# Prompt output summed in PSUM, gather from unscaled rows, and expert weights in transfers of 2 MB: a hybrid decoder step with a mixture of experts

## The reference, cut to what matters

```python
x = x + mix
x = x + moe(rmsnorm(x, norm_ffn_g), ...)     # then y = rmsnorm(x, norm_final_g)

logits = x2 @ w_router + b_router            # x2 is the normalised row, (288, 1024)
top_vals, top_idx = lax.top_k(logits, 4); gates = softmax(top_vals)
# rows sorted by expert, in blocks; each block with its expert's weights:
gu = xb @ w_up[e] + b_up[e]                  # w_up[e]: (1024, 2048)
gate, up = gu[:, :1024], gu[:, 1024:]
gate = minimum(gate, 7); up = clip(up, -7, 7)
act = (up + 1) * (gate * sigmoid(1.702 * gate))
out = act @ w_down[e] + b_down[e]            # w_down[e]: (1024, 1024)
y = segment_sum(out * row_gate, row_tok)
```

## Time and profile before

| what | value |
|---|---|
| runs | 1273.46 us median of 3 (1272.34 to 1274.46) |
| the profiled execution | 1271.02 us, with a span of 1269.2 us |
| busy | PE 1152.5 us (91%), DVE 676.7 (53%), POOL 653.9 (52%), ACT 244.0 (19%) |
| transfers | 448.91 MB (decimal), mean 354 GB/s over the span |
| mean granted clock of PE | 0.972 |

### The profile page before, as it was taken

One profiled execution on the slowest core, in us unless ns is written; L12 is line 12 of the kernel. 1 busy time (PEld: TensorE's weight loads), 2 busy tenths in 40 slices (PEclk: granted clock), 3 DMA queues, 4 the chain that ended last, 5 costly groups with the idle time before them and its releaser, 6 DMA issues.

```text
span 1269.2 us, 30932 instructions
## 1 busy us (share of the span) xinstructions
PE 1152.5 (91%) x11113; PEld 586.8 (46%) x11114; DVE 676.7 (53%) x1256; ACT 244.0 (19%) x487; POOL 653.9 (52%) x709
## 2 busy tenths in 40 slices
PE   8999999999999989799797998997997879979895
PEld 7777777775444334243332443432433324434332
DVE  2999984121755635545342557553554445535534
ACT  2012124001222212122121221221221212212122
POOL 1012300000566858749671687586585756857863
PEclk9999999999999999999898999998998989989998
DMA  9974443336999999999999799999999999999996
GB/s 263 349 242 129 163 129 117 114 142 278 380 385 397 396 422 422 421 422 422 422 422 422 282 400 424 422 422 422 422 422 422 422 422 422 422 422 422 422 422 277
DMA packets 94539, 448.91 MB, mean 354 GB/s; under 512 B 8502, under 2 KB 42870, under 8 KB 45315
## 3 DMA queue, kind: packets, MB, share of 16 engines
q1 hardware_dynamic: 94078, 447.21, 87.8%
q10 hardware_dynamic: 437, 1.39, 0.3%
HBM read 447.00 MB, written 2.42 MB: 354 GB/s over the span
## 4 chain that ended last, share of the span: by engine, by line
PE 60%; DMA 18%; DVE 17%; issue 3%; DVEq 1%; ACT 1%; POOL 0%; SPq 0%; POOLq 0%; ACTq 0%
PE banks L1372 21%; DMA ring<-in_w_down 17%; PE banks L1382 13%; DVE staging L803 8%; PE banks L1167 8%; PE banks L1089 5%; PE banks L1147 4%; PE banks L1126 3%; PE banks L1283 2%; PE banks L1133 2%; PE banks L1156 1%; DMA staging<-in_w_up 1%; DVE hT L1036 1%; DVE hT L1029 1%; DVE staging L812 1%
## 5 line engine op out<-in xcount | busy, mean ns | idle before, releaser
L524 POOL COPY ring<-staging 128x1024 f32<-128x1024 f32 x620 | 623.8, 1053 | 472.0 <-PE banks L1372 372.4
L1372 PE MATMUL banks<-ring,hT 128*32 128x512 f32 x3328 | 414.8, 604 | 12.7 <-DVE hT L779 7.5
L330 DVE TENSOR_TENSOR xt<-xt,banks 128x1024 f32<-128x1024 f32 x106 | 128.7, 1215 | 371.7 <-PE banks L1147 371.7
L1382 PE MATMUL banks<-ring,hT 128*32 128x256 f32 x3328 | 229.1, 395 | 73.3 <-DMA ring<-in_w_down 64.4
L1382 PEld LDWEIGHTS banks<-ring,hT 128*32 128x32 f32 x3328 | 109.6, 114 | 249.7 <-issue 136.3
L1167 PE MATMUL banks<-hT,ring 128*128 128x288 f32 x768 | 188.4, 406 | 0.3 <-ACT hT L561 0.3
L1372 PEld LDWEIGHTS banks<-ring,hT 128*32 128x32 f32 x3328 | 104.8, 111 | 149.9 <-issue 106.8
L1167 PEld LDWEIGHTS banks<-hT,ring 128*128 128x128 f32 x768 | 145.1, 190 | 39.7 <-issue 0.4
L683 ACT COPY WT<-banks 128x256 f32<-128x256 f32 x52 | 19.4, 372 | 533.8 <-PE banks L1382 533.8
L803 DVE SCALAR_TENSOR_TENSOR staging<-staging 128x256 f32<-128x256 f32 x240 | 107.4, 522 | 0.0
L762 DVE TENSOR_SCALAR WT<-slot_ids,prod 128x32 f32 x156 | 81.5, 581 | 0.0
(11 more groups left out here) (245 smaller groups left out, 737.0 us busy)
## 6 DMA issues: line engine op xcount, KB each, us to landing
staging<-in_w_up SPq DMA_DIRECT2D x248, 1024.0 KB, 18.5
ring<-in_w_down SPq DMA_DIRECT2D x66, 1024.0 KB, 11.1
staging<-in_w_down SPq DMA_DIRECT2D x62, 1024.0 KB, 18.4
ring<-in_w_in SPq DMA_DIRECT2D x24, 1024.0 KB, 10.3
ring<-in_w_up SPq DMA_DIRECT2D x8, 1024.0 KB, 4.8
ring<-in_w_branch_b SPq DMA_DIRECT2D x4, 1024.0 KB, 5.4
ring<-in_w_branch_a SPq DMA_DIRECT2D x4, 1024.0 KB, 4.9
ring<-in_w_out SPq DMA_DIRECT2D x4, 1024.0 KB, 5.0
```

Of the source, the lines that this page charges most:

```text
L330: nc.vector.tensor_tensor(dst, dst, rows, ALU.add).then_inc(y_added, 1)
L524: ins = nc.gpsimd.tensor_copy(ring[:, k, half], staged[k][:, half])
L1372: ins = mm(UP[g * BLK:(g + 1) * BLK, :], xT[:, k, :], ring[:, k, g * 512:(g + 1) * 512], start=k == 0, stop=k == UP_SLOTS - 1)
L1382: ins = mm(DN[q * BLK:(q + 1) * BLK, 0:256], actT[:, f % 4, f // 4, :], ring[:, UP_SLOTS + j, h * D + q * 256:h * D + (q + 1) * 256], star ...
```

## The change

1. **Transfers.** Two neighbouring slots become one unit of 2 MB, loaded by one transfer with runs of 16 KB: two rows of `w_up`, or four rows of `w_down`, for each partition. There are six units for an expert; units 0 to 4 go through `staging`, unit 5 (slots 10 and 11) is loaded into the ring. POOL still copies a slot at a time, from a unit that has landed whole; it counts 8 for each half on `unit_full`. SP's order is kept: units 0 to 2 of the place after, unit 5 of this place, units 3 and 4. Since a partition now holds rows 2p and 2p+1 of a unit, the transposes of the gathered rows take every second element, and those of `raw` and `b_up` every fourth; `norm_ffn_g` is loaded a second time, as four rows of 256, and turned into a ninth column set (`FFN_PAIRS`) for `take_x`.
2. **Prompt output.** Banks 4 to 7 hold the prompt's output through the whole expert loop. PE starts them with an identity times `xt` (`start_rows`), every `combine` adds to them, and the last one ends the sum. DVE's adds to `xt` and PE's waits for them leave; only the sample's add stays (`add_sample`). The tail's squares and scales read PSUM.
3. **Gather.** `stage` no longer holds scaled rows for the prompt: the 0/1 matrix is multiplied with the reciprocal, and the gather reads `xt`.

```diff
@@ staging @@
-        staged = [staging[:, u, h * SLOT:(h + 1) * SLOT] for u in range(STAGED) for h in range(2)]
+        staged = [staging[:, u, :] for u in range(STAGED)]
...
@@ sync @@
+            load(ffn_rows[:], a["norm_ffn_g"][0].rearrange("(q n) -> q n", q=QN), vec_in)
...
-            def load_slot(e, k):
-                sp.dma_start(ring[:, k, :], slot_source(e, k)).then_inc(slot_full[k], 16)
...
-            def load_last_slots(e, before):
-                for k in range(2 * STAGED, SLOTS):
-                    sp.wait_ge(down_used, before * DOWN_SLOTS + (k - UP_SLOTS + 1))
-                    load_slot(e, k)
+            def unit_source(e, u):
+                if u < UP_UNITS:
+                    return a["w_up"][0, bass.ds(e, 1), u * 256:(u + 1) * 256, :].rearrange("e (p h) n -> p (e h n)", p=P)
+                lo = (u - UP_UNITS) * 512
+                return a["w_down"][0, bass.ds(e, 1), lo:lo + 512, :].rearrange("e (p h) n -> p (e h n)", p=P)
+            def load_unit(e, u):
+                sp.dma_start(ring[:, 2 * u:2 * u + 2, :].rearrange("p s n -> p (s n)"), unit_source(e, u)
+                             ).then_inc(unit_full[u], 16)
+            def load_staged_again(place, after, us):
+                for u in us:
+                    sp.wait_ge(unit_full[u], place * 16 + 16)
+                    load_staged(after, u)
+            def load_last_unit(e, before):
+                sp.wait_ge(down_used, before * DOWN_SLOTS + DOWN_SLOTS)
+                load_unit(e, UNITS - 1)
...
-                load_staged_again(place, after, range(2 * AHEAD))
-                load_last_slots(here, before)
-                load_staged_again(place, after, range(2 * AHEAD, 2 * STAGED))
+                load_staged_again(place, after, range(AHEAD))
+                load_last_unit(here, before)
+                load_staged_again(place, after, range(AHEAD, STAGED))
@@ gpsimd @@
+                for u in range(UP_UNITS):
+                    pool.wait_ge(staged_full[u], place * 16)
+                    for h in range(2):
+                        pool.wait_ge(up_used, before * UP_SLOTS + (2 * u + h + 1))
+                        copy_slot(u, h)
...
@@ scalar, tail @@
+            act.wait_ge(rows_combined, 1)
             for tt in range(2):
-                act.wait_ge(y_added, bodies * NT + (NT + tt + 1))
-                nc.scalar.activation(stage[:, tt, :], xt[:, tt, :], ACT.Square, accum_out=ss[:, tt:tt + 1]
+                nc.scalar.activation(squares[tt], y_rows[tt], ACT.Square, accum_out=ss[:, tt:tt + 1]
                                      ).then_inc(squared3, 1)
-                act.wait_ge(squared3, tt + 1)
-                root(ss[:, 4 + tt:5 + tt], ss[:, tt:tt + 1], 1.0 / D, rooted2)
+            act.wait_ge(squared3, 2)
+            root(ss[:, 4:6], ss[:, 0:2], 1.0 / D, rooted2)
@@ vector @@
+                for tt in range(2):
+                    V.tensor_scalar(sel[:, tt, :], slot_ids[:, bass.ds(rank0, BLK)],
+                                    rankm[:, tt, bass.ds(expert, 1)], ss[:, 4 + tt:5 + tt], ALU.is_equal, ALU.mult)
...
-                    V.tensor_scalar(stage[:, tt, :], xt[:, tt, :], col2, None, ALU.mult).then_inc(rows_kept, 1)
...
-                add_before(i, 2)
+                add_sample(i)
                 dve.wait_ge(combT_turned, i + 1)
                 select_weighted(column1)
                 dve.wait_ge(gathered, i + 2)
                 select(column2)
-                add_before(i, 1)
-                dve.wait_ge(combined, i * NT + (NT + 1))
-                add_output(dve, row_out[0], 0)
@@ tensor @@
+                pairs = xg.rearrange("r (p h) -> r h p", h=2)
                 for h in range(2):
-                    ins = tr(turned[:, h], xg[:, h * P:(h + 1) * P])
+                    ins = tr(turned[:, h], pairs[:, h])
...
+            def start_rows():
+                for q in range(QN):
+                    mm(bank[4 + q].rearrange("p (t n) -> p t n", t=2), ident[:], x_cols[:, q], start=True, stop=False)
+            def combine(tt, last=False):
+                for q in range(QN):
+                    ins = mm(y_rows[tt][:, q, :],
                              combT[q * BLK:(q + 1) * BLK, tt * P:(tt + 1) * P],
-                             out_sb[q * BLK:(q + 1) * BLK, :], start=True, stop=True)
+                             out_sb[q * BLK:(q + 1) * BLK, :], start=False, stop=last)
...
-                pairs = raw.rearrange("t (b p h) -> t b h p", h=2, p=P)
+                fours = raw.rearrange("t (p c) -> t c p", c=4)
                 for c in range(4):
-                    ins = tr(TB[:, c * P:(c + 1) * P], pairs[:, c // 2, c % 2])
+                    ins = tr(TB[:, c * P:(c + 1) * P], fours[:, c])
...
                 for k in range(UP_SLOTS):
-                    up(k, after)
+                    up(k, after + 8, after + 16)
                     if k == 2:
                         pe.wait_ge(act_ready, i + 1)
-                        pe.wait_ge(y_added, i * NT + 2)
+                        pe.wait_ge(sample_added, i + 1)
                     if 2 <= k < 2 + DOWN_SLOTS:
-                        down(k - 2, here)
+                        down(k - 2, here + 8, here + 16)
                 pe.wait_ge(combT_ready, i + 2)
                 pe.wait_ge(out_ready, i + 1)
-                pe.wait_ge(y_added, i * NT + NT)
-                combine(0, row_out[0])
+                combine(0)
```

More of the change, by code:

```diff
@@ L185, in carve @@
             return regs[region][0:rows, lo:lo + n]
+        squares = [regs["hT"][:, tt * D:(tt + 1) * D].rearrange("p (q n) -> p q n", q=QN) for tt in range(2)]
         xT = carve("hT", KC * BLK).rearrange("p (k t) -> p k t", k=KC)
@@ L213, in hybrid_layer @@
         UP, TB, XB, DN = bank[0:4]
[L214 to L217, removed]
+        high = banks[:, 4:8, :]
+        y_rows = (high[:, :, 0:256], high[:, :, 256:512])
+        sample_out = DN[:, 256:512]
         slot_full = [sem(f"slot_full{k}") for k in range(SLOTS)]
-        staged_full = [sem(f"staged_full{k}") for k in range(2 * STAGED)]
+        unit_full = [sem(f"unit_full{u}") for u in range(UNITS)]
+        staged_full = [sem(f"staged_full{u}") for u in range(STAGED)]
         slot_free = sem("slot_free")
@@ L390, in _ @@
                 load_block(n)
[L392 to L397, removed]
-            def load_slot(e, k):
-                sp.dma_start(ring[:, k, :], slot_source(e, k)).then_inc(slot_full[k], 16)
-            def load_staged(e, k):
-                sp.dma_start(staged[k], slot_source(e, k)).then_inc(staged_full[k], 16)
@@ L428, in _ @@
-            for k in range(UP_SLOTS, 2 * STAGED):
-                load_staged(1, k)
+            for u in range(UP_UNITS, UNITS):
+                load_unit(0, u)
+            load_staged(1, STAGED - 1)
             sp.wait_ge(before_known, 1)
@@ L1095, in _ @@
                 if tt == 1:
-                    pe.wait_ge(vec_in, 16 * 8)
-                    tr(bank[7][:, 320:320 + 8 * KC], vecrows).then_inc(pe_early, 1)
+                    pe.wait_ge(vec_in, 16 * 9)
+                    tr(bank[7][:, 320:320 + 8 * KC], vecrows)
+                    pairs = ffn_rows[:].rearrange("q (p h) -> q h p", h=2)
+                    turned = bank[7][:, 320 + 8 * KC:320 + 9 * KC].rearrange("p (q h) -> p h q", h=2)
+                    for h in range(2):
+                        ins = tr(turned[:, h], pairs[:, h])
+                    ins.then_inc(pe_early, 1)
                 r = ROWS[tt]
@@ L1374, in up, with down @@
                 ins.then_inc(up_used, 1)
-            def down(j, fills):
-                pe.wait_ge(slot_full[UP_SLOTS + j], fills)
+            def down(j, half, full):
+                if j < 3:
+                    pe.wait_ge(unit_full[UP_UNITS + j // 2], half if j == 0 else full)
                 for h in range(2):
@@ L1456, in _ @@
             pe.wait_ge(act_ready, bodies + 1)
-            pe.wait_ge(y_added, bodies * NT + 2)
+            pe.wait_ge(sample_added, bodies + 1)
             for j in range(DOWN_SLOTS):
-                down(j, last)
+                down(j, last + 8, last + 16)
             pe.wait_ge(combT_ready, bodies + 2)
             pe.wait_ge(out_ready, bodies + 1)
-            pe.wait_ge(y_added, bodies * NT + NT)
-            for tt in range(2):
-                combine(tt, tail_out[tt])
-            pe.wait_ge(y_added, bodies * NT + (NT + 1))
-            tr(Y0[:, 256:384], ident[:])
-            combine_sample(Y0[:, 256:512])
+            combine(0)
+            combine(1, last=True).then_inc(rows_combined, 1)
+            combine_sample()
             pe.wait_ge(quarters_squared, 2)
-            pe.wait_ge(y_added, bodies * NT + (NT + 2))
             sum_quarters(UP[:, 0:1])
```

169 lines of the change are left out of this document (81 added, 88 removed).

## The result

The changed kernel takes 1282.16 us (median of six runs, 1280.81 to 1285.9) beside 1274.51 us for the kernel before on the same chip: a ratio of 1.0063, 95% interval 1.0052 to 1.0075. It is **slower by some 8 us**, and the forecast, 1279.1 with a range of 1270 to 1287, holds. The profiled execution took 1281.75 us with a span of 1279.9, 10.7 us more than the profiled one of before, which was faster than each of the six runs of before that the ratio rests on (1272.34 to 1275.87).

What follows compares the result with a forecast made beforehand. Weight transfers bound the long expert stretches, PE's own pace the time between. Start +2.4, restarts +3.4, bytes -9.2, dry queue +6.6 and end +2.4 sum to +5.6 us: 1279.1 for the median, range 1270 to 1287.

Steps and rivals of the forecast that it cites:

- DVE's adds: Expert blocks: removing L330's 106 adds, 128.7 us of DVE, saves 0, since nothing was behind them.
- The strides: PE's transposes: changed element strides cost 0; far ends 0.1 us less or 0.3 us more a block.
- The rival of a shorter block: PE's block loses up to 0.4 us and SP's releases come sooner: -4.3 us, 1269.2; chance 0.17.
- Start: Before the expert loop: ninth vector +0.3, matmuls starting the four output banks +2.1; together +2.4 us.
- Restarts: SP at L401 with the queue dry: the 2 MB unit goes out 1.7 us later, at two places, +3.4 us.
- The bytes: Full stretches: 16 KB runs take 2.447 us per MB instead of 2.485, 428.5 GB/s; -9.2 us.
- The rate rival: Full stretches: the rate stays near 422 GB/s; sum +11.9 us, 1285.4; chance 0.20.
- The queue runs dry in six cycles: Behind L401's release: 1.0 us of work left against a 2.1 us restart, dry 1.1 us six times, +6.6 us.
- the rival without it: Expert cycles: the queue doesn't run dry; sum -1.0 us, 1272.5, no change; chance 0.18.
- End: Last expert and tail: the last up waits for two copies, +2.0, and the new tail +0.4; together +2.4 us.
- The two copies: Before the last up: unit 3 lands whole, so it waits for two POOL copies, not one; +2.0 us.
- The new tail: After the last combines: three DVE adds leave, but both squares wait for both combines; +0.4 us.

Runs made afterwards that it cites:

- e4: The changed kernel with the same 2 MB units, but rows laid out as before, in runs of 8 KB instead of 16 KB: ratio to before 1.0082.
- e1: The kernel before with only the PSUM-summed prompt output, gather from xt and new tail; transfers stay at 1 MB: ratio to before 1.0011.
- e3: The changed kernel with only the last unit split into two 1 MB transfers, each released and awaited by itself: ratio to before 0.9952.
- e7: e3 with both halves of the last unit issued only at the fourth down slot, each still awaited by itself: ratio to before 0.9964.
- e5: The kernel before with the first of the two last w_down slots released at the fourth down slot instead of the third: ratio to before 1.0016.
- e10: e3 with PE waiting for both halves of the last unit before it uses the first; releases as in e3: ratio to before 1.0025.
- e12: e3 with two of the four banks' start matmuls moved into the place of dummy matmuls before the first up: ratio to before 0.9954.
- e6: The kernel before with 2 MB units, the last split into two 1 MB transfers; DVE adds the output as before: ratio to before 0.9951.

## Why the prediction was right, and where its sizes were off

The span cut at PE's waits puts the two profiles side by side. The forecast column is the recorded sum's terms, laid on the same cuts (a stretch's first wait now ends with the fourteenth megabyte instead of the thirteenth, 14 x 2.447 - 13 x 2.485 = +1.95).

| stretch | before | after | difference | forecast |
| --- | --- | --- | --- | --- |
| first up to first long wait's end | 120.72 | 126.44 | +5.7 | 2.1 + 1.7 + 1.95 = +5.8 |
| to the fourth's end (96 MB, two dips) | 238.63 | 238.06 | -0.6 | -3.65 + 2.2 = -1.4 |
| to the next stretch's first | 101.58 | 106.05 | +4.5 | 1.7 + 1.95 = +3.7 |
| to the last one's end (168 MB, four dips) | 417.58 | 416.07 | -1.5 | -6.4 + 4.4 = -2.0 |
| to the last up | 39.63 | 40.12 | +0.5 | -3.0 + 2.0 = -1.0 |
| to the end | 21.80 | 23.54 | +1.7 | +0.4 |

The first up came at 329.26 and 329.62 (forecast +0.3), which says little, since it lies between 329.3 and 332.2 in the profiles here. The first stretch came out as forecast. Of the others all went the forecast way but the last up's, and each came out 0.5 to 1.5 us worse: +10.7 in all, not +5.6. Between the medians of the runs it is +7.7. By step:

- **DVE's adds: 0.** Right. L330 is gone, and a pair of blocks takes 31.74 us between releases (477.12 to 508.86) against 31.71. The 0 was in part two small terms that cancel. Idle before L1130 halved to 6.2 us, some 0.1 us a block. The strides, though, which the prediction read as free, are not: six transposes of a block take 1.07 us, before and in e4 1.00, and the shortest weight load from hT went from 138 to 194 ns. The rival of a shorter block falls.
- **Start.** Right: 2.12 us reached the release (e1), forecast 2.1. That it is so near is luck: the eight instructions took 3.70 us, not 3.4, and 1.6 of them were covered, not 1.3.
- **Restarts: 1.7 each.** Right at the first: the release after the dry queue came 89.49 us after the first up, 1.8 later than e1's 87.69, and its unit was awaited whole. At the second it came 69.1 us behind the wait that ended at 694.12, before 66.7 behind 688.61: 2.4 later.
- **The bytes.** Right to 0.001 us: 2.447 us per MB forecast, 58.74/24 = 2.448 measured, and e4 showed that it is the run. The rate rival falls. The Trainium skill, "DMA: Bandwidth & Descriptors", section "Bandwidth", has 425 GB/s for its largest transfer, one of 16 MB issued from GpSimd; in this trace, with transfers of SP queued behind each other, 24 MB in 58.74 us are 428.4 GB/s over a whole cycle, and the measurement decides. What the prediction worked out from 425 is a little off: with its own terms the sum comes out some 3.5 us later, not 3.8.
- **The queue runs dry in six cycles.** Right in mechanism, place and number; the rival without it falls. It measured 8.1 us, not 6.6. The sum had set a dip at the release's distance from the wait's end, less 50.9 us (53.8 - 0.8 - 2.1), and had the release at 52.0. It came at 52.80, 52.27, 52.96, 52.41, 51.80 and 51.76. That gives dips of 1.9, 1.4, 2.1, 1.5, 0.9 and 0.9 us; the six cycles were 1.7, 1.5, 2.1, 1.2, 0.7 and 1.0 too long. So the rule holds cycle by cycle, and the term that was mis-sized is the distance, 52.3 in the mean. It was read from one cycle of before, and it changes with how long PE runs at half its clock behind the wait. In the changed kernel, behind the wait that ended at 456.06, and then over 16 us behind those that ended at 800.17 and 1038.37:

```profile
456.00:460.00 4.00, 3.94 (x32) 1.45 (x36) 0.00 (x0) 0.00 (x0) 0.10 (x1) 0.50 1.00 426
460.00:461.00 1.00, 1.00 (x16) 0.48 (x12) 0.00 (x0) 0.00 (x0) 1.00 (x2) 0.54 1.00 426
461.00:462.00 1.00, 1.00 (x16) 0.33 (x12) 0.00 (x0) 0.68 (x2) 0.92 (x1) 1.00 1.11 475
...
800.17:816.17 16.00, 16.00 (x157) 6.44 (x161) 4.03 (x13) 3.61 (x7) 6.02 (x7) 0.83 1.01 428
1038.37:1054.37 16.00, 15.81 (x175) 6.57 (x179) 4.03 (x13) 3.52 (x7) 7.09 (x8) 0.91 1.01 428
```

  PE ran at half its clock for 4.9 us behind the first of these, and by the mean clocks for some 5.4 and 2.9 behind the others, whose releases are the latest and one of the two earliest of the six. The length of the wait doesn't tell them apart: PE had been idle for 6.77 us before 800.17 and for 7.60 before 1038.37. Behind the cycle that the forecast was read from the earlier trace rows it was 3.4 us. The release is one of the things that this moves, and the third row of the table is another.
- **End.** The two copies cost what was forecast: POOL's last pair began at 1252.31 and the last up at 1256.36, 4.05 us later against 2.07 before. Two things were missed. The issue at 1237.53 met a queue near its end too (356 GB/s over 1238 to 1242), so the last 14 MB took 36.1 us, not 34.3. And the final downs ran at half clock for the larger part (0.69 in the mean):

```profile
1256.36 1.06 PE L1381 MATMUL banks<-ring,hT 128*32 128x512 f32 x8 [0.85 <-POOL ring L519]
...
1263.21 5.24 PE L1392 MATMUL banks<-ring,hT 128*32 128x256 f32 x64 [2.58 <-DVE xq L1046]
```

  5.24 us where before took 3.66. The new tail itself costs nothing, not 0.4: in e3, at full clock, the last up to the end is 21.72 us, beside 21.80 before.

What a unit of 2 MB costs is thus taken apart. The late release alone costs little (e7, e5). The late landing alone costs most: in e10 7.1 us in the cycles, where the changed kernel has 8.1, and some 9 us in all (1.0025, against 0.9952 of e3 and 0.9954 of e12 on e10's own chip). Both together cost some 14 to 17 (1.0063 and 1.0082 against 0.9952). The last pair of numbers is the changed kernel, whose last unit is also one transfer with longer runs; two halves with both the late release and the late landing were not run. My forecast had put both into one margin, which is right for the sum; that the landing weighs more was not in it. Why the rate recovers so slowly in e10 stays open.

## What to carry to other kernels

A larger transfer is two changes in one: longer runs, which raised the rate by 1.5% here exactly as the price per run said, and a coarser grain of release and landing, which cost more than that wherever the queue's reserve at the release was less than a restart (here 1.0 us of work by the forecast's count, against 2.1). Take the first without the second: keep the large pieces, and split only the one that a compute engine waits for and that gates the issues behind it (0.9952 instead of 1.0063 to 1.0082). Measure such a loop by the distance between the ends of its long waits; that distance counts bytes, and it resolved 0.1 us where the kernel's time, over a dozen runs, did not resolve 2.

## What was not expected of the hardware

- A DVE operation of at most 1.11 us (L1029 in the profile of before) took 5 to 7 us in sixteen places of three profiles, all from one chip, each time beside an unbroken row of POOL's copies of 1 us, and PE waited for it. The Trainium skill, "SBUF — State Buffer", section "SBUF: two separate sides", has GpSimd and some DVE operations (those in a two-port mode, and those with two inputs from SBUF) take a pair of ports under an exclusive lock, held for one whole instruction, while the other engine is blocked. The waits here agree with a lock, but last through several of POOL's instructions (6.98 us, some six copies), longer than that rule says; which mode L1029 ran in the traces don't show. Why it came in those three profiles only stays open; e6, from the same chip, had none.
- The final 64 downs took 3.66, 5.1 to 5.4, or about 6.5 us, by the granted clock: its mean times the duration is 3.6 or 3.7 us in each (1.00 x 3.66 in e3, 0.55 x 6.58 in e12). The idle time ahead doesn't tell them apart (2.30 us in e3, 2.35 in e12). An edit that moves the tail can lose or gain 2.9 us there.
